# The per-channel gates of two residual layers: spread over the partitions by TensorE instead of by a trip through HBM

## The reference, cut to what matters

```python
for l in range(2):
    mod = silu_c @ w_mod[l] + b_mod[l]           # 2048 -> 3 * 2048
    shift, scale, gate = jnp.split(mod[:, None, :], 3, axis=-1)
    cshift, cscale, cgate = jnp.split(silu_cc @ w_mod[l] + b_mod[l], 3)
    ...                                          # two attention mixers -> y, yc
    x = x + gate * (y @ w_o[l])
    if l == 0:
        cx = cx + cgate * (yc @ w_o[l])
```

## Time and profile before

| | |
|---|---|
| median of 3 runs (lowest, highest) | 2590.6 us (2589.32, 2591.97) |
| the profiled execution, time | 2590.6 us |
| the profiled execution, span from first to last instruction | 2588.8 us |
| PE busy | 2486.0 us, 96% of the span, 12220 matmul records |
| DVE, ACT, POOL busy | 1219.7, 1036.1, 217.1 us |
| mean granted clock of PE | 0.987 of full speed |
| DMA | 467.97 MB, mean 181 GB/s |

### The profile page before, as it was taken

The page is one execution under the profiler, slowest core; times in us unless marked ns, Lnnn a source line. Parts: engine busy times, 40 slices in busy tenths (PEclk is TensorE's granted clock), DMA queues, the critical chain, the costliest instruction groups (busy, mean ns, idle before and its releaser), DMA issues. The chain is left out here.

```text
span 2588.8 us, 31901 instructions
## 1 busy us (share of the span) xinstructions
PE 2486.0 (96%) x12220; PEld 1940.1 (75%) x12220; DVE 1219.7 (47%) x2104; ACT 1036.1 (40%) x1722; POOL 217.1 (8%) x308
## 2 busy tenths in 40 slices
PE   6789999999999999999989999999999999999998
PEld 2456788877777667776777678977888888889886
DVE  1121244445554322352555556576576544444664
ACT  2122323334443312252344345544554545664543
POOL 0000101011110000000212100001020001111200
PEclk8889999999999999999999999999999999999999
DMA  8656733333332577557536445666575566667653
GB/s 324 230 198 241 246 98 111 97 118 112 92 90 80 200 268 248 196 181 251 174 125 193 135 152 191 209 210 185 167 215 174 187 208 208 189 184 228 195 191 130
DMA packets 230535, 467.97 MB, mean 181 GB/s; under 512 B 16986, under 2 KB 41880, under 8 KB 229104
## 3 DMA queue, kind: packets, MB, share of 16 engines
q1 hardware_dynamic: 209104, 394.94, 47.3%
q0 software_dynamic: 21280, 70.99, 8.7%
HBM read 435.06 MB, written 30.80 MB: 180 GB/s over the span
## 5 line engine op out<-in xcount | busy, mean ns | idle before, releaser
L1933 PE MATMUL pp<-w_hi,hT_hi 128*128 128x512 f32 (+3 forms) x2904 | 1179.3, 406 | 27.8 <-DVE w_lo L1372 25.4
L1935 PE MATMUL pp<-w_hi,hT_lo 128*128 128x512 f32 (+3 forms) x2904 | 1120.7, 386 | 0.0
L1934 PE MATMUL pp<-w_lo,hT_hi 128*128 128x512 f32 (+3 forms) x2904 | 1119.0, 385 | 0.0
L1372 DVE TENSOR_TENSOR w_lo<-raw,w_hi 128x1024 fp32r<-128x1024 f32 (+4 forms) x570 | 671.9, 1183 | 820.2 <-ACT w_hi L1100 818.9
L1100 ACT ACTIVATE w_hi<-raw 128x1024 fp32r<-128x1024 f32 (+4 forms) x570 | 579.4, 1023 | 487.8 <-PE pp L1935 254.0
L1933 PEld LDWEIGHTS pp<-w_hi,hT_hi 128*128 128x128 f32 x2904 | 550.7, 190 | 205.4 <-issue 79.2
L1935 PEld LDWEIGHTS pp<-w_hi,hT_lo 128*128 128x128 f32 x2904 | 549.1, 189 | 106.5
L1934 PEld LDWEIGHTS pp<-w_lo,hT_hi 128*128 128x128 f32 x2904 | 551.4, 190 | 94.9 <-issue 7.2
L1253 ACT ACTIVATE arena<-pY 128x512 f32<-128x512 f32 (+2 forms) x114 | 62.1, 545 | 149.0 <-PE pY L2080 115.0
L913 POOL DMA_DIRECT2D scratch_u<-ust x46 | 33.7, 733 | 885.0 <-ACT ust L1162 884.9
L2093 PEld LDWEIGHTS pO<-arena 128*128 128x128 f32 x640 | 85.4, 191 | 11.1 <-issue 3.4
(11 more groups left out here) (282 smaller groups left out, 1648.9 us busy)
## 6 DMA issues: line engine op xcount, KB each, us to landing
raw<-in_w_mod_dram SPq DMA_DIRECT2D x192, 512.0 KB, 4.9
raw<-in_w_in_dram SPq DMA_DIRECT2D x168, 512.0 KB, 4.2
raw<-in_e_w_in_dram SPq DMA_DIRECT2D x104, 512.0 KB, 3.9
raw<-in_w_o_dram SPq DMA_DIRECT2D x64, 512.0 KB, 4.9
raw<-in_o_w_in_dram SPq DMA_DIRECT2D x64, 512.0 KB, 4.5
raw<-in_w_out_dram SPq DMA_DIRECT2D x64, 512.0 KB, 3.8
raw<-in_w_in_dram SPq DMA_DIRECT2D x56, 440.0 KB, 4.0
scratch_u<-ust POOLq DMA_DIRECT2D x35, 512.0 KB, 4.2
```

The costliest lines, as they stand in the source:

```text
L1372: dve.tensor_tensor(w_lo[:, g.s % SPLIT, 0:n], raw[:, g.n % RAW, 0:n], w_hi[:, g.s % SPLIT, 0:n].bitcast(F32), ALU.subtract).then_inc(lo_d ...
L1933: pe.matmul(dst, hT_hi[:, kk, o:o + P], hi[:, k, :], start=a, stop=False)
L1934: pe.matmul(dst, hT_hi[:, kk, o:o + P], lo[:, k, :], start=False, stop=False)
L1935: ins = pe.matmul(dst, hT_lo[:, kk, o:o + P], hi[:, k, :], start=False, stop=z)
```

## The change

The scratch tensor for the gates, its eight stores and its eight spreading loads go. In their place PE multiplies the selector rows (2 rows x 128 columns, stationary) by the two gate rows (2 x 512, moving) in float32: the result is 128 equal rows of the latent gate in bank `X0`, and in layer 0 also of the context gate in bank `O`. ACT copies the bank or banks to `gateB` (in the diff, the first added `gate` is ACT's, the second PE's). The event `gate` moves from just after the start of the chunk to eight slots before its end (slots 566, 614, 662, 696 in layer 0 and 948, 964, 980, 996 in layer 1). DVE's evacuation waits for ACT's copy instead of for the DMA, and ACT's copy of the layer-1 rows waits for PE's use of the layer-0 rows instead of for the stores.

```diff
             if ch.kind == "mod":
-                if ch.row is not None:
-                    add(ch.q1 + 6, "gate_store", ch.name)
...
                 if ch.layer < 2:
-                    add(max(ch.q0 + 1, C[f"out{ch.layer}_{int(ch.name[-1]) - 1}"].q1 + 3 if ch.name[-1] != "0" else 0), "gate", ch.name)
+                    add(ch.q1 - 8, "gate", ch.name)
...
+                elif name == "gate":
+                    take("X0", *e)
+                    if self.W.C[key[0]].T == 4:
+                        take("O", *e)
...
-            def gate_store(name):
-                ch = C[name]
-                r = 32 * ch.row
-                pool.wait_ge(*freed_from("O", ("cols", name)))
-                pool.dma_start(dram["gates"][4 * ch.layer + ch.row], rows[r:r + 2, :]).then_inc(gate_stored, 16)
-
-            def gate(name):
-                ch, n = C[name], int(name[-1])
-                if n:
-                    prev = C[f"{name[:-1]}{n - 1}"]
-                    pool.wait_ge(*freed_from(prev.bank[-1], ("acc", prev.name, prev.T - 1)))
...
-                pool.wait_ge(gate_stored, 64 * (ch.layer + 1))
-                T = ch.T // 2
-                pool.dma_start(gateB[:, 0:T, :], dram["gates"][4 * ch.layer + n, 0:T, :].partition_broadcast(P)).then_inc(gate_here, 16)
...
                 if ch.layer == 1:
-                    act.wait_ge(gate_stored, 64)
+                    act.wait_ge(filled["X0"], left["X0", ("gate", f"out0_{ch.row}")])
+                    act.wait_ge(filled["O"], left["O", ("gate", f"out0_{ch.row}")])
...
+            def gate(name):
+                n = int(name[-1])
+                ch = C[name]
+                if n:
+                    prev = C[f"{name[:-1]}{n - 1}"]
+                    act.wait_ge(*freed_from(prev.bank[-1], ("acc", prev.name, prev.T - 1)))
+                for v, b in enumerate(("X0", "O")[:ch.T // 2]):
+                    act.wait_ge(filled[b], left[b, ("gate", name)])
+                    act.activation(gateB[:, v, :], bank[b], ACT.Copy).then_inc(freed[b], 1)
...
-                    dve.wait_ge(gate_here, 16 * nth["gate", name])
+                    dve.wait_ge(*freed_from(("X0", "O")[v], ("gate", name)))
...
+            def gate(name):
+                ch, n = C[name], int(name[-1])
+                l = ch.layer
+                r = 32 * n
+                pe.wait_ge(*freed_from("O", ("cols", f"gate{l}_{n}")))
+                for v, name_ in enumerate(("X0", "O")[:ch.T // 2]):
+                    b = begin(name_, "gate", name)
+                    c = C_ROW + 128 * v
+                    pe.matmul(b, keep[r:r + 2, c:c + 128], rows[r:r + 2, :], start=True, stop=True).then_inc(filled[name_], 1)
```

More of the change, by code:

```diff
@@ L635, in build @@
         "u0": [512, EVEN1], "u1": [512, ODD1], "u2": [256, EVEN2], "u3": [256, ODD2],
-        "uq": [256, 1536], "ukv": [512, 2048], "decay": [8, 256], "gates": [8, 2, 512]}.items()}
+        "uq": [256, 1536], "ukv": [512, 2048], "decay": [8, 256]}.items()}
     weights = {"w_mod0": D["w_mod"][0], "w_mod1": D["w_mod"][1], "e_w_in": D["e_w_in"][0], "o_w_in": D["o_w_in"][0],
@@ L685, in build @@
         x_again, cleared = sem("x_again"), sem("cleared")
-        gate_stored, gate_here = sem("gate_stored"), sem("gate_here")
         x_hi, y_hi, lat_hi = sem("x_hi"), sem("y_hi"), sem("lat_hi")
@@ L1069, in _ @@
                         store(*key)
[L1070 to L1073, removed]
                     elif name == "tables":
@@ L1351, in _ @@
             mine = {"evac": evac, "cols": cols, "sq_x": sq_x, "sq": sq, "sq_x2": sq_x2, "x_turn": x_turn, "y_turn": y_turn, "lat_turn": lat_turn,
-                    "front_copy": front_copy, "exp": exp, "copy": copy, "squares": squares, "kpe_turn": kpe_turn,
+                    "gate": gate, "front_copy": front_copy, "exp": exp, "copy": copy, "squares": squares, "kpe_turn": kpe_turn,
                     "i_turn": i_turn, "ik_turn": ik_turn, "i_dots": i_dots, "g_soft": g_soft, "g_exp": g_exp,
@@ L2161, in fl_sum @@
                 pe.matmul(b[0:8, 128:256], fl[:, 1, :], tri_le, start=False, stop=True).then_inc(filled["Y"], 1)
-            mine = {"gains": gains, "cols": cols, "x_turn": x_turn, "y_turn": y_turn, "lat_turn": lat_turn, "kpe_turn": kpe_turn,
+            mine = {"gains": gains, "cols": cols, "gate": gate, "x_turn": x_turn, "y_turn": y_turn, "lat_turn": lat_turn, "kpe_turn": kpe_turn,
                     "front_k": front_k, "front_q": front_q, "score": score, "turn": turn_, "pv": pv, "i_turn": i_turn, "ik_turn": ik_turn,
```

## The result

The changed kernel takes 2610.2 us (median of 6 runs, 2606.41 to 2611.0), the kernel before 2589.89 us (6 runs): a ratio of 1.0075, with a 95% interval of 1.0063 to 1.0087. It is 20.3 us slower, where 13 were forecast. The time lies 1.2 us above the range. The profiled execution of the changed kernel is the slowest on record, 2614.76 us with a span of 2613.0.

A forecast was written before the change was run, and what follows sets the result against it. PE was taken to bound the kernel; 2590.6 us plus 13.4 us of added matmuls (4 x 2.11 + 4 x 1.25), other terms 0, less some half a us of swallowed idle, gave 2603.5 us; range 2597 to 2609.

The forecast's parts named there:

- What bounds the kernel: Whole kernel: PE-bound, busy 2486.0 of 2588.8 us; 1.5 us of idle in the stages touched; HBM trip wholly hidden.
- Removed: 16 DMA issues on POOL, 8.6 us together, and 3 MB of loads: worth 0, bound -1.1 us.
- Added on PE: 12 float32 matmuls at eight slots: 2.11 us per layer 0 visit, 1.25 per layer 1 visit; 13.4 us, bounds 10.3 to 15.0.
- the new wait: Rival, chance 0.06: late ACT copy in `out0_3` makes PE stand at layer 1's start, perhaps slower clock behind; 2609 us.
- if the clock falls anew near a visit: Sign in the profile after that would show the prediction wrong; the matmuls were priced without any clock loss.
- Does PE wait: At the eight visits PE waits neither for the gate rows nor for banks `X0` and `O`: 0.
- Added on ACT: 12 copies of 128x512 from PSUM, 6.5 to 7.5 us on an engine 60% idle; no split held up: 0.
- Moved: DVE's deadline, now a copy eight slots before chunk end; tightest at `out0_3` with slack 1.6 us: 0.
- Given back later: After the visits: nothing absorbed beyond 1.5 us; the stall in 1250 to 1350 keeps its size, later by 8 us.
- the dearer pair: Rival, chance 0.12: each matmul of a pair pays full price, or array-part changes cost more for two rows; 2606 to 2609.
- The hidden work: Rival, chance 0.10: new PE work at the visits partly hidden in short gaps; 2597 us.
- the faster case: Rival, chance 0.04: DMA and queue relief brings weights and layer 1's first mixer sooner, saving over 13.4 us; 2585 us.

The follow-up runs named there:

- no gates at all: Neither path against the kernel before: no stores, loads, spreading matmuls or copies, output chunks multiplied by x instead of the gate; 2589.96 us, ratio 1.0003.
- the matmuls alone: The kernel before with its HBM trip kept, plus the twelve two-row matmuls at the same slots, banks freed without a copy; 2610.59 us, ratio 1.008.
- the changed kernel again: The changed kernel unaltered, run again for a second trace; 2611.76 us, ratio 1.0088 to the kernel before.
- 32 rows: The changed kernel with each gate matmul fed the 32-row block that holds the gate's two rows, thirty of them zero; 2603.59 us, ratio 1.0059.
- three in a row: The full-height form with three matmuls instead of two per layer 0 visit, the context gate's row being spread twice; 2604.4 us, ratio 1.0054.
- split: The changed kernel with layer 0's context gate matmul moved four slots ahead of the latent gate's; 2606.88 us, ratio 1.0068.
- 64 rows: The full-height form cut to the block of 64 rows that holds the gate's two; 2605.7 us, ratio 1.0067.
- full-height form: The changed kernel with gate matmuls using all 128 rows: a repeated identity column times the whole zeroed `rows` tile; 2601.01 us, ratio 1.0046.

## Why the prediction was wrong, point by point

*What bounds the kernel* and *Removed*: right. With no gates at all the time is the same within its interval, and PE's busy time too (2485.8 us against 2486.0).

*Added on PE*: the bounds and the rows were well chosen. 2.12 us for a pair and 1.26 for a single, against 2.11 and 1.25; going to a part of the array and back costs 0.40 us for two rows (2.12 - 2 x 0.86), where 64 rows had 0.39. That is the drain which TensorEngine Tiling (Array Packing) of the Trainium skill ("Key Properties") names; the traces agree with it.

*The failed step* is in the same part: the sum priced the matmuls by their time alone, with the clock left at 1.00. I read "PE busy, clock 1.00" in the stretch and took it that more busy time would leave it so. A pair of two-row matmuls is busy time that didn't keep the clock. This term, 4 x 1.6 to 1.7 = about 6.5 us with four falls and 5.4 at 13 falls for 16 pairs, was missing from the sum and from the range. The clock was named twice, as the tail of the new wait (chance 0.06), behind an idle PE, and in the list of what would make the prediction wrong ("if the clock falls anew near a visit"). It fell without any wait. The trace before held no matmul with so few rows, so the price was not there to be read; what could be read was that the two-row case was outside everything measured, and that called for a wider range upward.

*Does PE wait, Added on ACT, Moved*: right. PE's idle time in 943 to 1260 of the trace after is one wait of 0.6 us, as before; line 1389 waits for PE only; the copies take 0.60 us; the matmuls alone give the whole loss.

*Given back later*: right that nothing is given back. The stall after 1250 moved by 15.0 us (1254.02 against 1238.97), where 8 were forecast, since the falls come on top, and it swallowed nothing: 100 - 85.45 = 14.6 us of idle in 1266 to 1366 against 13.3. But the part put this stretch at no cost, and it has one. The distance that is 248.39 us in the trace before, from layer 1's last `cols` to the matmul at 1487.36, is 249.2 to 252.8 us in all ten traces with added matmuls, and 247.9 in the kernel without gates. Some of it is single falls, but the three traces that have none between 1280 and 1400 us (the changed kernel again, 32 rows, three in a row) still lose 1.3 to 1.6 us. This term is smaller than the first, and it rests on one trace of the kernel before.

*The rivals*: the dearer pair came to 2606 to 2609, near the result, for a reason that wasn't its own. The hidden work and the faster case fell with the 22.2 us of added busy time and with the kernel without gates.

*What stays open.* The medians of the variants lie 1 to 3 us over the sum of their visits (split: 17.9 over the kernel before against 15; 64 rows: 16.7 against 13.4). In size the stretch just named would account for it, but the medians are of other executions than the traces, so this isn't shown; nor why work added before that stretch makes it longer. Single falls between 1280 and 1400 us come and go between traces, also in the kernel without gates; whether the added work makes them more frequent, one trace of each kernel can't tell. Nor was it tried how many rows between 2 and 32 are enough. Why few rows matter to the clock, and whether it is their number alone or also the values in them, no run shows.

## What to carry to other kernels

In this kernel, which is bound by PE, the hidden DMA trip was free, and its replacement by matmuls cost their full stream of columns, however few rows they had. If PE must do such a small job, try its matmul with more rows, even rows of zeros (4 to 11 us less here), or big matmuls between two of them (2 to 5 us less), and look at the granted clock in stretches of a few us behind each visit: tenths over fortieths of a span hide it.

## What the runs showed of the hardware that was not expected

- Two float32 matmuls in a row with 2 rows, 128 columns and 512 moving columns (1.9 us from the first to the next big matmul) were followed by 3.4 us at half clock in 14 of 20 cases (13 of 16 in layer 0, 1 of 4 in layer 1), with PE busy throughout. The same two with 32 rows: 0 of 4, at the same durations; with 64 rows 0 of 4, with 128 rows 0 of 8 (four of them with three in a row).
- A float32 matmul of 512 columns costs 0.86 us with 128 rows and 1.25 to 1.26 with 64 or 2 rows of the array, when it stands alone between full ones. For the eight visits of this change that is 3 us (13.5 against 10.3, by the sum of the visits); the full-height form measured 2.5 us under the one with 32 rows.
